# Five of the eight input products of the last attention are cut into parts and run between the attention's steps

## The reference

```
q, k, v, z = split(u @ w_in, 4)            # four products 512x1024 by 1024x1024
q = q.reshape(b, s, 8, 2, 64) * 64**-0.5   # 8 heads, two maps of 64 each
k = k.reshape(b, s, 8, 2, 64);  v = v.reshape(b, s, 8, 128)
block of 128 queries:
    sc = q . k + bias(distance)            # per head and per map, causal
    p  = softmax(where(dist >= 0, sc, NEG))
    a  = p[map 0] - lam * p[map 1]
    o  = a @ v
o = rmsnorm(o, subln) * (1 - lambda_init)
out = (o * silu(z)) @ w_out                # 512x1024 by 1024x1024
```

## Time and profile before

| | |
|---|---|
| median of 3 runs | 2195.23 us |
| the profiled execution | 2195.47 us, its span 2194.2 us |
| mean granted clock of TensorE | 0.989 of full speed |
| PE matmul busy | 2102.6 us, 96% of the span |
| DVE, ACT, POOL busy | 1002.4, 780.6, 254.5 us |
| chain that ended last | PE 84%, DVE 7%, ACT 5% |
| last layer, first product to the end of the attention | 1906 to 2132 us |

### The profile page before, as it was taken

How to read it: one execution, slowest core, us unless ns; L and a number is a source line. 1 busy time by engine, 2 the same in 40 slices (tenths; PEclk the granted TensorE clock), 3 DMA queues, 4 the chain that set the end, 5 groups by cost and what they waited for, 6 DMA issues and landing times.

```text
span 2194.2 us, 26569 instructions
## 1 busy us (share of the span) xinstructions
PE 2102.6 (96%) x10149; PEld 1717.0 (78%) x10149; DVE 1002.4 (46%) x2026; ACT 780.6 (36%) x1485; POOL 254.5 (12%) x360
## 2 busy tenths in 40 slices
PE   6998999999999999999999999989989999899978
PEld 4887887888888885888888888767878888688656
DVE  4437433443354336355544333545255553522575
ACT  4326332222232223332422222333265553332562
POOL 0103000000001110000100000010025552000340
PEclk9999999999999999999999999999999999999999
DMA  4330242333233330332333333253221112333211
GB/s 156 108 99 11 68 118 88 96 96 96 87 115 106 96 96 10 96 97 87 106 96 96 96 96 96 68 154 109 77 76 43 35 35 97 108 96 96 78 39 49
DMA packets 96765, 190.46 MB, mean 87 GB/s; under 512 B 8407, under 2 KB 16639, under 8 KB 96512
## 3 DMA queue, kind: packets, MB, share of 16 engines
q1 hardware_dynamic: 90288, 164.35, 24.7%
q0 software_dynamic: 6352, 24.41, 3.4%
HBM read 184.48 MB, written 4.26 MB: 86 GB/s over the span
## 4 chain that ended last, share of the span: by engine, by line
PE 84%; DVE 7%; ACT 5%; issue 2%; POOL 1%; DMA 0%; ACTq 0%; DVEq 0%; SPq 0%; POOLq 0%
PE bank L672 65%; PE bank L708 7%; PE bank L1097 3%; PE bank L940 2%; PE bank L1078 2%; DVE wl L1749 1%; ACT junk L1266 1%; DVE hTl L1821 1%; PE bank L1067 1%; DVE xn L1811 1%; PE bank L925 1%; PE bank L1010 1%; PE bank L1068 1%; PE bank L744 1%; PE bank L1104 1%
## 5 line engine op out<-in xcount | busy, mean ns | idle before, releaser
L1749 DVE TENSOR_TENSOR wl<-raw,wh 128x1024 fp32r<-128x1024 f32 x306 | 375.5, 1232 | 833.6 <-ACT wh L1227 833.2
L1227 ACT ACTIVATE wh<-raw 128x1024 fp32r<-128x1024 f32 x306 | 321.3, 1054 | 899.0 <-PE bank L672 875.0
L672 PE MATMUL bank<-hTh,wh 128*128 128x512 f32 (+1 forms) x1328 | 517.3, 390 | 0.2 <-issue 0.2
L672 PE MATMUL bank<-hTl,wh 128*128 128x512 f32 (+1 forms) x1328 | 516.7, 389 | 0.0
L672 PE MATMUL bank<-hTh,wl 128*128 128x512 f32 (+1 forms) x1328 | 516.6, 389 | 0.0
L672 PEld LDWEIGHTS bank<-hTh,wh 128*128 128x128 f32 (+1 forms) x1328 | 247.9, 187 | 53.5 <-issue 0.3
L672 PEld LDWEIGHTS bank<-hTh,wl 128*128 128x128 f32 (+1 forms) x1328 | 247.9, 187 | 53.2
L672 PEld LDWEIGHTS bank<-hTl,wh 128*128 128x128 f32 (+1 forms) x1328 | 248.0, 187 | 53.0
L672 PE MATMUL bank<-wh,hTh 128*128 128x512 f32 x464 | 181.6, 391 | 2.5 <-DVE hTl L2449 2.4
L672 PE MATMUL bank<-wh,hTl 128*128 128x512 f32 x464 | 180.6, 389 | 0.0
L672 PE MATMUL bank<-wl,hTh 128*128 128x512 f32 x464 | 180.6, 389 | 0.0
(11 more groups left out here) (357 smaller groups left out, 2766.7 us busy)
## 6 DMA issues: line engine op xcount, KB each, us to landing
raw<-in_ffn_w_in SPq DMA_DIRECT2D x88, 512.0 KB, 3.7
raw<-in_ret_w_in SPq DMA_DIRECT2D x48, 512.0 KB, 3.8
raw<-in_ffn_w_out SPq DMA_DIRECT2D x44, 512.0 KB, 3.7
raw<-in_diff_w_in SPq DMA_DIRECT2D x32, 512.0 KB, 3.7
raw<-in_fox_w_in SPq DMA_DIRECT2D x24, 512.0 KB, 3.8
raw<-in_nsa_w_in SPq DMA_DIRECT2D x20, 512.0 KB, 3.6
raw<-in_ret_w_out SPq DMA_DIRECT2D x16, 512.0 KB, 3.7
bt<-bias_by_lag POOLq DMA_DIRECT2D x16, 448.0 KB, 3.9
```

The costliest lines, as they stand in the source:

```text
L672: i = pe.do.matmul(dst, x, y, start=first and k == 0 and q == 0, stop=stop)
L1227: act.do.activation(M.hl[n % HL_SLOTS][0][:, 0:m], M.raw[n % RAW_SLOTS][:, 0:m], ACT.Copy).then_inc(*T.up("act_hi", n))
L1749: dve.do.tensor_tensor(wl[:, 0:m], M.raw[n % RAW_SLOTS][:, 0:m], wh[:, 0:m].bitcast(F32), ALU.subtract).then_inc(*T.up("dve_lo", n))
```

## The change

PE now makes v0, q0 and k0 as before, one after the other. The other five products (q4, k4, v1, z0, z4 in this order) are cut into 16 units each. A unit is one output tile and one chunk: six matmuls. The 80 units are dealt out at 2.45 per attention step, so they run in steps 0 to 32. Within a product the tile is now the outer loop and the chunk the inner one, so all four chunks are used for each tile, and a chunk is released only in the last tile. Tiles alternate between banks 6 and 7. ACT and DVE take a finished tile, and make the splits (in the last tile), at the end of their own part of the same step.

The attention now has one bank for transposes (4, before 4 and 5) and one for the product with V (5, before 6 and 7). The turn stands three steps behind the scores and the product with V four (before four and six). ACT copies z without Silu, and applies Silu to Z in SBUF after the loop, in four instructions of 128 x 1024, ahead of the square root. The five products v1, z0, z4, q4 and k4 no longer call `banks4`, five calls fewer.

```diff
-    for b in (4, 5, 6, 7, 0, 2, 1, 3):
+    for b in (4, 0, 2, 1, 3, 5, 6, 7):
         block8("diff", (b * 512, 512))
...
+DIFF_FILL = [("diff q4", "F"), ("diff k4", "F"), ("diff v1", "T"), ("diff z0", "F"), ("diff z4", "F")]
+DIFF_STEPS = 32 + 5
+def fill_parts(n):
+    total = 16 * len(DIFF_FILL)
+    return range(min(total, int(n * 2.45)), min(total, int((n + 1) * 2.45)))
...                                           # pe_diff
-    pe_product(pe, T, M, "diff v1", "T", 8, h_, ready, 512, dve_frees("dve_out", "diff v1"))
     b = T.bank["diff subln"] = pe.banks4()[0]
...
+    pe_product(pe, T, M, "diff q0", ...)
+    pe_product(pe, T, M, "diff k0", ...)
+    base = pe.use
+    pe.use += 4 * len(DIFF_FILL)
+    def fill(u):
+        (tag, mode), o, c = DIFF_FILL[u // 16], u % 16 // 4, u % 4
+        b, n, cols = 6 + o % 2, base + u // 16 * 4 + c, slice(o * 128, o * 128 + 128)
+        if c == 0:
+            pe_bank(pe, T, b)
+        pe_weights(pe, T, n)
+        ...                                   # the six matmuls of a unit
+        if c == 3 or o == 3:
+            i.then_inc(*up("pe_product", *[(tag, o)] * (c == 3), *[("chunk", n)] * (o == 3)))
...
-        b, buf, i = 4 + n % 2, d.rows[n % 6], n % 4      # turn
+        b, buf, i = 4, d.rows[n % 6], n % 4
...
-        b = 6 + h % 2                                    # after
+        b = 5
...
+    for n in range(DIFF_STEPS):
         if n < 32:
             scores(n)
+        if 0 <= n - 3 < 32:
+            turn(n - 3)
         if 0 <= n - 4 < 32:
+            after(n - 4)
+        for u in fill_parts(n):
+            fill(u)
...                                           # act_diff: z by Copy, fill() at the end of each step, then
+    for k in range(0, 8, 2):
+        act.do.activation(d.Z[:, k:k + 2, :], d.Z[:, k:k + 2, :], ACT.Silu)
...                                           # dve_diff: fill(), after the joins of the step
+        if 0 <= n - 5 < 32:
+            after(n - 5)
+        for u in fill_parts(n):
+            fill(u)
```

More of the change, by code:

```diff
@@ L1146, in pe_diff @@
     pe.free[b] = [("dve_sub", "subln")]
[L1147 to L1151, removed]
-    T.note("pe", "diff heads")
+    pe_product(pe, T, M, "diff q0", "F", 8, h_, ready, 512, dve_frees("act_out", "diff q0"))
+    pe_product(pe, T, M, "diff k0", "F", 8, h_, ready, 512, dve_frees("dve_out", "diff k0"))
+    T.note("pe", "diff heads")
+    base = pe.use
+    pe.use += 4 * len(DIFF_FILL)
+    taken = {"q": "act_out", "k": "dve_out", "v": "dve_out", "z": "act_z"}
+    def fill(u):
+        (tag, mode), o, c = DIFF_FILL[u // 16], u % 16 // 4, u % 4
+        b, n, cols = 6 + o % 2, base + u // 16 * 4 + c, slice(o * 128, o * 128 + 128)
+        T.bank[tag] = [6, 7, 6, 7]
+        if c == 0:
+            pe_bank(pe, T, b)
+        wh, wl, nk = chunk_views(M, n)
+        pe_weights(pe, T, n)
+        for k in range(nk):
+            kk = c * nk + k
+            for name, key in ready(kk, None):
+                pe.wait_ge(*at(name, key))
+            h, l = M.HTh[:, kk, :], M.HTl[:, kk, :]
+            if mode == "F":
+                parts = [(wh[:, k, cols], h), (wh[:, k, cols], l), (wl[:, k, cols], h)]
+            else:
+                parts = [(h[:, cols], wh[:, k, :]), (h[:, cols], wl[:, k, :]), (l[:, cols], wh[:, k, :])]
+            for q, (x, y) in enumerate(parts):
+                end = k == nk - 1 and q == 2
+                i = pe.do.matmul(M.bank[b][:, :], x, y, start=kk == 0 and q == 0, stop=c == 3 and end)
+        if c == 3 or o == 3:
+            i.then_inc(*up("pe_product", *[(tag, o)] * (c == 3), *[("chunk", n)] * (o == 3)))
+        if c == 3:
+            pe.free[b] = [(taken[tag[5]], (tag, o))]
     def scores(n):
         h, i = n // 4, n % 4
-        L, base, o = 128 * (i + 1), 4 * (h // 4), h % 4
+        L, first, o = 128 * (i + 1), 4 * (h // 4), h % 4
         for m in range(2):
@@ L1659, in act_diff, with take_z, take_q, fill @@
     act.do.activation(d.lam[:, 2:4], d.lam[:, 0:2], ACT.Exp).then_inc(*up("act_lam", "exp"))
[L1661 to L1678, removed]
+    def take_z(tag, o):
+        act.wait_ge(*at("pe_product", (tag, o)))
+        act.do.activation(d.Z[:, int(tag[-1]) + o, :], M.bank[bank[tag][o]][:, :], ACT.Copy).then_inc(*up("act_z", (tag, o)))
+    def take_q(tag, o):
+        act.wait_ge(*at("pe_product", (tag, o)))
+        act.do.activation(d.qT[:, int(tag[-1]) + o, :], M.bank[bank[tag][o]][:, :], ACT.Copy, scale=0.125).then_inc(
+            *up("act_out", (tag, o)))
+    def fill(u):
+        (tag, _), o, c = DIFF_FILL[u // 16], u % 16 // 4, u % 4
+        if c == 3 and tag[5] == "q":
+            take_q(tag, o)
+        if c == 3 and tag[5] == "z":
+            take_z(tag, o)
+        if o == 3:
+            act_split(act, T, M)
+    act_product(act, T, M, 4, 4, lambda o: take_q("diff q0", o))
+    act_product(act, T, M, 4)
     T.note("act", "diff heads")
@@ L2335, in dve_diff, with take_v, take_k, fill @@
     at, up, d, bank = T.at, T.up, M.diff, T.bank
[L2337 to L2352, removed]
+    def take_v(tag, o):
+        half = int(tag[-1])
+        stage_begins(dve, T, "nsa")
+        dve.wait_ge(*at("pe_product", (tag, o)))
+        dve.do.tensor_copy(d.V[:, o, half * 512:half * 512 + 512], M.bank[bank[tag][o]][:, :]).then_inc(*up("dve_out", (tag, o)))
+    def take_k(tag, o):
+        dve.wait_ge(*at("pe_product", (tag, o)))
+        dve.do.tensor_copy(d.kT[:, int(tag[-1]) + o, :], M.bank[bank[tag][o]][:, :]).then_inc(*up("dve_out", (tag, o)))
+    def fill(u):
+        (tag, _), o, c = DIFF_FILL[u // 16], u % 16 // 4, u % 4
+        if c == 3 and tag[5] == "k":
+            take_k(tag, o)
+        if c == 3 and tag[5] == "v":
+            take_v(tag, o)
+        if o == 3:
+            dve_split(dve, T, M)
+    dve_by_tile(dve, T, M, lambda o: take_v("diff v0", o), late=("n5", {1: (2,), 2: (3,)}))
     dve.wait_ge(*at("ldlq", "lq"))
@@ L2421, in dve_diff @@
             join(n - 2)
-        if 0 <= n - 6 < 32:
-            after(n - 6)
+        if 0 <= n - 5 < 32:
+            after(n - 5)
+        for u in fill_parts(n):
+            fill(u)
     v, y, a, o = (d.ocell[:, c, :] for c in range(4))
@@ L2442, in dve_diff @@
         dve.wait_ge(*at("dve_sub", "subln"))
[L2443 removed]
+        dve.wait_ge(*at("act_silu", ("diff z", k)))
         if k >= 2:
```

38 lines of the change are left out of this document (17 added, 21 removed).

## The result

The changed kernel takes 2198.33 us (median of 16 runs, 2194.26 to 2200.80) against 2194.37 us for the kernel before, timed beside it (16 runs, 2191.62 to 2198.91). The ratio is 1.0016, 95% interval 1.0008 to 1.0023. Its profiled execution took 2198.99 us, with a span of 2197.7 us and a mean granted clock of 0.982. Against the profiled execution of before (2195.47 us) that is 3.5 us more; 2.8 were predicted.

The account below looks back on a forecast made before the run. It took the attention to be bound by a ring of short steps over four engines, none full. Terms -10.2 + 5.2 + 7.5 + 0.3 = +2.8 us on 2195.47 gave 2198.3 us, range 2193.5 to 2205.

Parts of the forecast that it names:

- Filling the gaps and the end of the loop: Five products plus attention, to ACT's copy of the last head: 181.9 us before, 171.7 now, a gain of 10.2 us.
- Going from attention to products and back costs nothing extra: On PE, switching adds nothing to the attention's own work, put at 6.8 us per head, 54.6 us for eight.
- The wait for v1: In step 20 PE waits about 2.2 us for DVE's copy of V's last tile, queued behind a low part.
- The end of the loop: From the last unit's end E to ACT's last copy: E+8.2 us, 5.1 of it waits; join 31 at E+4.8.
- Silu: Between ACT's last square and the square root, a table load and four instructions add 5.2 us.
- The drain: Rival at ACT's table switch: a drain is paid after all, 1.4 us more, 2199.7 us; chance 0.05.
- The banks: Output product's first half moves to banks 4 to 7 and waits for DVE's multiplications with Z: 7.5 us more.
- The clock on top: First output-product matmuls at half clock after the gap ahead of bank 4: 0 to 1.3 us, taken as 0.3.
- Point (4) of what would show it: After the transposed heads PE idles about 8 us, with gaps before the second to fourth tile, ended by DVE's multiplication.
- The slip at each border: Rival in the loop: ACT's splits delay Exp, turns wait, 9 us lost instead of 3: 2204.3 us; chance 0.22 with long low clock.
- Gaps that fill without loss: Rival in the loop: no waits at borders and a tail at its lower bound, 2193.7 us; chance 0.13.
- The banks' rival: At the output product the wait for the second half is covered, 7.5 + 0.3 us go: 2190.5 us; chance 0.05.

Follow-up runs that it names:

- e12: e4 with ACT's copies of the transposed block and copy and square of a head put ahead of Exp in each step: 2178.84 us, 0.9936 to before.
- e3: Changed kernel with the bank halves turned once more ahead of the output product and Silu moved behind the square root: 2187.10 us, 0.9967 to before.
- e8: Changed kernel with DVE's last two low parts of step 32 moved behind join 31: 2195.55 us, 1.0003 to before.
- e6: Kernel before with z copied in the products and Silu applied at the end, ahead of the square root: 2199.49 us, 1.0023 to before.
- e2: Changed kernel with the four Silu instructions moved behind the square root: 2193.14 us, 0.9998 to before.
- e5: Kernel before with one more turn of the bank halves ahead of the output product: 2201.47 us, 1.0035 to before.
- e7: Changed kernel with 24 unused identity matmuls on PE between the transposed heads and the output product: 2200.11 us, 1.0020 to before.
- e4: e3 with units dealt out as 48 in steps 0 to 18 and 32 in steps 19 to 34: 2179.41 us, 0.9938 to before.
- e1: Changed kernel with one more turn of the bank halves ahead of the output product: 2190.36 us, 0.9988 to before.
- e11: Changed kernel with 48 units dealt out in steps 0 to 18 (2.53 each), then 2.45 per step again: 2198.73 us, 1.0030 to before.

## Why the prediction was right

The predicted 2198.3 us stands against 2198.33 measured, and the verdict against before (+0.16%, interval 0.08 to 0.23%) is the likeliest case, "within 0.2%". The mechanism held in the main: all four terms (loop, Silu, banks, clock) are there, at the places and for the reasons given. That the two times agree to 0.03 us is luck. The step that was predicted is +2.8 us; measured are +4.0 between the medians and +4.2 over the stages. The 1.2 to 1.4 us that are missing are hidden by the kernel before, whose median beside the changed one is 2194.37, 1.1 us below the profiled 2195.47 from which the sum started. The terms, with what the runs showed:

- **Filling the gaps and the end of the loop: -10.2 predicted, -9.2 measured.** The loop took 172.6 us for 171.7. PE's own work was put too low and the waits at the inner borders too high. A head of four steps without a wait (steps 24 to 27, first score matmul to first score matmul) takes 2089.54 - 2068.88 = 20.66 us. Its 60 product matmuls at 0.227 are 13.6 of them, so the attention's part is 7.06 and not 6.8 us, 1.9 us more in eight heads: "Going from attention to products and back costs nothing extra" did not hold. e12, with no wait left, takes 166.0 us in all where the sum has 109.0 + 54.6 = 163.6 for the work. The waits inside were put at 3.0 us; v1 took 1.7, and the waits listed above show none at the other three borders.
- **The wait for v1: 2.2 predicted, 1.7 in the trace** (from 2048.5 to 2050.24), at the step and for the reason given: the copy of V's last tile behind the low part behind ACT's split. Not foreseen: the half clock that follows it in some traces, 1.6 us more (e3).
- **The end of the loop: E+8.2 predicted, E+8.3 measured.** Join 31 ended at E+4.05, not E+4.8, since DVE had less backlog; the half clock cost 1.2 us over the last seven blocks with V (3.19 against 2.01 in e8) and 0.4 over the last four transposes (1.09 against 0.66), together 1.6 and not 0.8. Two errors that cancel.
- **Silu: +5.2 predicted, +5.2 measured** in after, e6 and, with the sign turned, in e2. The drain (a rival, 0.05) is refuted.
- **The banks: +7.5 for the wait, 7.4 measured** (e5; e7 and e8, with less of the half clock, give the same). **The clock on top: 0.3 predicted, 0.8 to 0.9 measured** (after against e7 and e8), within the 0 to 1.3 given.
- **Point (4) of what would show it was half wrong.** The gap ahead of bank 4 is there (6.6 us, ended by DVE's multiplication). The gaps before the second to fourth tile are not: the 14 half-clock matmuls fill them. The prediction had this at six matmuls. The sum hardly moves, for the last tile then ends at 2153.0 instead of some 2152.0; the picture in the trace does.
- **The rivals.** The slip at each border (2204.3) did not happen: the only joins that PE waits for are the last two, 30 and 31. Gaps that fill without loss (2193.7) came out only once the fill had been moved (e4, e12). The banks' rival (2190.5, chance 0.05) took the wait for the banks as covered. It wasn't; e1 takes it away, by other means, and the stage gives back 8.3 us where the rival had 7.8.

Where did the gain go? Gaps of PE worth up to 18.3 us by the prediction's sum were there; 9.2 were won and 13.5 were given back behind the loop, by two things that have nothing to do with the gaps: an instruction group put ahead of the root on ACT, and the parity of a counter. Undoing both gives -0.33% (e3). Dealing the units out another way as well gives -0.62% (e4), and with ACT's order changed it is -0.64% (e12).

Open: what decides whether the clock falls behind the wait of 1.7 us; and the steps of 1 to 3 us in earlier layers, which no kernel here was made to look at.

## What to carry to other kernels

When independent work is interleaved with a chain, look first at what the order of each in-order queue puts ahead of the chain's next instruction where that work ends: all waits in the loop stood at such borders, and the engines that PE waited for were busy about half of the time (DVE 85.4 and ACT 82.6 of 171.9 us). A counter that hands out buffers in turn is part of the interface: with two halves, as here, taking an odd number of calls away moves every later user, so compare buffer numbers, not only lines, before and after an edit. And when a shift of the schedule removes one wait, look at the next border before counting the gain (e11).

## What the runs showed of the hardware

- A filler of 24 products of 128 columns held the granted clock at 1.00 for its 5.5 us, and it still fell to 0.50 four matmuls into the product behind it (2.15 us of idle time between). Keeping PE busy in this wait moved and shortened the half clock, and didn't remove it.
- The same wait of 1.7 us was followed by the half clock in three traces (e2, e3, e8) and not in three others (after, e1, e7), with the same instructions around it.
- At the half clock matmuls of 512 columns are 0.427 us apart, at the full clock 0.227.
- A table load took 1.28 us behind Square (before, after), behind Sqrt (e2) and behind Silu (after, e6), and the next instruction started 0.01 to 0.02 us after it each time.
- Silu of 128 x 1024 from SBUF to SBUF: four in 3.89 us, 0.97 each with their overlap. The Copy of the same size is no faster: three in 2.94 us, 0.98 each (e11).
